# Attention in a two-layer backbone kernel: the weighted values of two query tiles in one fp32 product of 256 columns, turned probabilities in four places

## The reference

```
def block(qblk):
    s = jnp.einsum('bhgqd,bhkd->bhgqk', qblk, k_all).astype(jnp.float32) * scale
    pr = jax.nn.softmax(s, axis=-1).astype(v_all.dtype)
    return jnp.einsum('bhgqk,bhkd->bhgqd', pr, v_all)
...
y = jnp.concatenate([multiscale_pool(p[..., :D_POOL], pool_w, pool_scale), attn], axis=-1) @ w_out
```

## Time and profile before

| | us |
|---|---|
| time of three runs, median (lowest to highest) | 1564.88 (1564.79 to 1565.66) |
| time of the profiled execution | 1565.75 |
| its span (first to last instruction) | 1564.0 |
| PE busy in the span | 1544.2 |
| DVE busy | 1047.2 |
| ACT busy | 572.4 |
| attention stage, scores of tile 1 to the last weighted values | 1075.2 to 1155.5 |

### The profile page before, as it was taken

One profiled execution on the slowest core, in us unless ns is written; L12 is line 12 of the kernel. 1 busy time (PEld: TensorE's weight loads), 2 busy tenths in 40 slices (PEclk: granted clock), 3 DMA queues, 4 the chain that ended last, 5 costly groups with the idle time before them and its releaser, 6 DMA issues. The chain is left out here.

```text
span 1564.0 us, 21770 instructions
## 1 busy us (share of the span) xinstructions
PE 1544.2 (99%) x8590; PEld 1325.1 (85%) x8590; DVE 1047.2 (67%) x1567; ACT 572.4 (37%) x870; POOL 24.3 (2%) x66
## 2 busy tenths in 40 slices
PE   8999999999999999999999999998999999999998
PEld 5888888778898888888888888988988888888887
DVE  4999999888848784678626446877647543444346
ACT  5423224684722221122211225635646332322233
POOL 0000000220000000000000000000000000000000
PEclk9999999999999999999999999999999999999999
DMA  9632132125136453445333223340022323233232
GB/s 323 198 80 81 55 109 67 68 83 147 34 111 220 161 189 121 149 162 195 113 100 129 55 91 71 107 140 28 1 68 68 95 93 117 72 107 108 81 99 89
DMA packets 132746, 171.54 MB, mean 110 GB/s; under 512 B 16114, under 2 KB 88498, under 8 KB 132666
## 3 DMA queue, kind: packets, MB, share of 16 engines
q1 hardware_dynamic: 131770, 168.25, 33.7%
q0 software_dynamic: 640, 2.10, 0.3%
q10 hardware_dynamic: 256, 0.08, 0.0%
HBM read 166.17 MB, written 2.15 MB: 108 GB/s over the span
## 5 line engine op out<-in xcount | busy, mean ns | idle before, releaser
L741 PE MATMUL acc<-h_hi,w_hi 128*128 128x512 f32 (+1 forms) x1424 | 494.5, 351 | 0.0
L741 PE MATMUL acc<-h_lo,w_hi 128*128 128x512 f32 (+1 forms) x1424 | 492.4, 349 | 0.0
L741 PE MATMUL acc<-h_hi,w_lo 128*128 128x512 f32 (+1 forms) x1424 | 492.3, 349 | 0.0
L1757 DVE TENSOR_TENSOR w_lo<-raw,w_hi 128x1024 fp32r<-128x1024 f32 x183 | 218.1, 1219 | 131.9 <-ACT w_hi L1257 131.7
L741 PEld LDWEIGHTS acc<-h_hi,w_lo 128*128 128x128 f32 x1424 | 267.1, 189 | 35.0
L741 PEld LDWEIGHTS acc<-h_hi,w_hi 128*128 128x128 f32 x1424 | 267.3, 189 | 34.5
L741 PEld LDWEIGHTS acc<-h_lo,w_hi 128*128 128x128 f32 x1424 | 267.2, 189 | 33.8
L1257 ACT ACTIVATE w_hi<-raw 128x1024 fp32r<-128x1024 f32 x183 | 186.5, 1053 | 216.3 <-PE acc L790 150.7
L790 PE MATMUL acc<-w_hi,hid_hi 128*128 128x512 f32 x434 | 169.5, 391 | 0.0
L790 PE MATMUL acc<-w_hi,hid_lo 128*128 128x512 f32 x434 | 168.9, 389 | 0.0
L790 PE MATMUL acc<-w_lo,hid_hi 128*128 128x512 f32 x434 | 168.8, 389 | 0.0
(11 more groups left out here) (300 smaller groups left out, 2067.8 us busy)
## 6 DMA issues: line engine op xcount, KB each, us to landing
ada_w<-in_ada_w SPq DMA_DIRECT2D x96, 512.0 KB, 5.7
raw<-in_ffn_w_in SPq DMA_DIRECT2D x88, 512.0 KB, 3.6
raw<-in_ffn_w_out SPq DMA_DIRECT2D x44, 512.0 KB, 4.4
raw<-in_even_w_in SPq DMA_DIRECT2D x24, 512.0 KB, 4.5
ada<-in_ada_w SPq DMA_DIRECT2D x8, 1024.0 KB, 12.0
raw<-in_odd_w_in SPq DMA_DIRECT2D x12, 512.0 KB, 3.7
raw<-in_even_w_out SPq DMA_DIRECT2D x8, 512.0 KB, 5.9
raw<-in_odd_w_out SPq DMA_DIRECT2D x8, 512.0 KB, 4.0
```

The source lines that it names most:

```text
L741: last = nc.tensor.matmul(acc[:, s, m, t0:t1], w[:, slot, kk, c], x_[:, k, t0:t1], start=(k == 0 and q == 0), stop=(k == KD - 1 and q == 2))
L1757: return nc.vector.tensor_tensor(out_, in0, in1, op)
```

## The change

`weighted_values(n)` becomes `weighted_pair(p)`, which multiplies tiles 2p and 2p + 1 together: six fp32 products of 256 columns, whose streamed operand is two pieces of 128 columns from two neighbouring places of `pT`. It is issued only in even rounds from 2 on (pair n/2 - 1 behind the transposes of tile n), and once behind the loop. Odd rounds have none. `pT` gets four places, at another offset, and `turned_copy` and `head_high` wait by pairs. DVE's program, ACT's order and everything else are as they were.

```
-        pT = place("pT", [P, 2, T], offset=A0 + 74624)
+        pT = place("pT", [P, 4, T], offset=A0 + 52096)
...
-            def weighted_values(n):
-
-                hd, i = divmod(n, NL)
-                pe.wait_ge(sem("pT_ready"), n + 1)
+            def weighted_pair(p):
+
+                hd, i = divmod(2 * p, NL)
+                pe.wait_ge(sem("pT_ready"), 2 * p + 2)
                 if hd >= 2 and i == 0:
                     pe.wait_ge(h_ready, HEADS + hd - 1)
-                c = (hd % 2) * 512 + i * P
+                c, b = (hd % 2) * 512 + i * P, 2 * (p % 2)
+                dst = acc[:, 1, 1, c:c + 2 * P].rearrange("p (a t) -> p a t", t=P)
                 for j in range(NT):
-                    last = nc.tensor.matmul(acc[:, 1, 1, c:c + P], v1[:, j, (hd // 3) * HD:(hd // 3 + 1) * HD],
-                                            pT[:, n % 2, j * P:(j + 1) * P], start=(j == 0), stop=(j == NT - 1))
-                if n < N_Q * NL - 1:
+                    last = nc.tensor.matmul(dst, v1[:, j, (hd // 3) * HD:(hd // 3 + 1) * HD],
+                                            pT[:, b:b + 2, j * P:(j + 1) * P], start=(j == 0), stop=(j == NT - 1))
+                if p < N_Q * NL // 2 - 1:
                     last.then_inc(sem("pv_done"), 1)
                 return last
...
-                if n >= 1:
-                    weighted_values(n - 1)
-            last = weighted_values(N_Q * NL - 1)
+                if n >= 2 and n % 2 == 0:
+                    weighted_pair(n // 2 - 1)
+            last = weighted_pair(N_Q * NL // 2 - 1)
...
-                    act.wait_ge(sem("pv_done"), NL * (hd + 1))
+                    act.wait_ge(sem("pv_done"), NL // 2 * (hd + 1))
...
-                if n >= 2:
-                    act.wait_ge(sem("pv_done"), n - 1)
-                nc.scalar.activation(pT[:, n % 2, :], acc[:, 1, 0, 0:T], ACT.Copy).then_inc(sem("pT_ready"), 1)
+                if n >= 4:
+                    act.wait_ge(sem("pv_done"), n // 2 - 1)
+                nc.scalar.activation(pT[:, n % 4, :], acc[:, 1, 0, 0:T], ACT.Copy).then_inc(sem("pT_ready"), 1)
```

## The result

The changed kernel takes 1571.35 us (median of 6 runs, 1571.2 to 1571.81), the kernel before 1565.04 us beside it (1564.75 to 1565.66). The ratio is 1.004, with a 95% interval of 1.0029 to 1.005: slower by 6.3 us. The forecast was 1571.2 us.

The account below looks back on a forecast made before the run. PE was taken to bound the attention stage. Waits of 3.9 us in the middle, with the width's gain included, 1.25 at the start and 1.15 at the end summed to +6.3 us: 1571.2 us, range 1568.8 to 1573.5.

Parts of the forecast that it names:

- The rule of 2.18 us: Attention stage: the next transposes can start 2.18 us after the last ones started, through DVE, if scores stood directly ahead.
- The three terms: Attention stage: PE loses 3.9 us in the middle, 1.25 us at the start and 1.15 us at the end.
- the two chains: From one set of transposes to the next: 2.18 us through DVE's normalisation, 1.80 us through ACT's turned copy.
- the boldest single step: Stage start: tile 2's transposes wait for ACT's turned copy of tile 1, so start at 1084.24 in both kernels.
- The width: Weighted values: a pair in 256-column products takes 2.59 us instead of 2.68, 1.1 us gained over twelve pairs.
- The size of the waits in the profile: PE waits: nine of 0.4 to 0.5 us, about 1.5 us at tile 22, about 1.7 us at tile 2.
- Rival 1: Even transposes: DVE's chain fits, ACT's does not, leaving 0.09 us waits in the middle; 1567.3 us, chance 0.06.
- Rival 2: Whole stage: all waits are hidden and only the width counts; 1563.8 us, chance 0.04.
- Rival 3: Waits cost more: slow two-piece operand (up to +1.1 us) or a clock fall at the start (1575 us); chance 0.06.

Follow-up runs that it names:

- the exchange on DVE: Changed kernel with DVE normalising each even tile before taking the maximum of the next odd tile: 1567.15 us, ratio 1.0014.
- the one product put between: Changed kernel with one of a pair's six products moved between odd and even transposes, and head_high one round later: 1567.10 us, ratio 1.0014.
- the longer maximum: One more maximum on DVE per tile, over 384 of the scores: 1576.75 us in the changed kernel, 1567.03 us in the kernel before.
- the order alone: Changed kernel's order and four pT places, but weighted values again as products of 128 columns: 1572.39 us, ratio 1.0048.

## Why the prediction was right

**The rule of 2.18 us** was its centre, and the trace gives 2.19 (1107.71 to 1109.90). That DVE's order sets it is shown by the exchange on DVE, by the one product put between, and by the longer maximum, which costs nearly three times as much in one order as in the other.

**The three terms** can be read off the two chains. They are measured between ends of weighted values, in both traces, and the stage's beginning is taken out by counting from its first scores (1075.20 before, 1074.73 after).

| | predicted | before, us | after, us | difference |
|---|---|---|---|---|
| start of tile 2's transposes, from the first scores | same | 9.04 | 9.03 | 0.0 |
| from there to the end of the next weighted values | +1.25 | 2.19 | 3.44 | +1.25 |
| middle, to the end of the weighted values of tile 19 | +3.9 | 54.92 | 58.89 | +3.97 |
| end, to the last weighted values | +1.15 | 14.13 | 15.30 | +1.17 |
| sum | +6.3 | 80.28 | 86.66 | +6.4 |

The first scores came 0.47 us earlier in the trace of the changed kernel (1074.73), a difference from ahead of the stage, and behind the last weighted values both have the same rest (408.5 and 408.6 us). Hence the spans differ by 6.0 and not 6.4 us. That the forecast time missed the median by only 0.15 us is in part luck: the kernel before alone gave medians of 1564.88 to 1565.11 us, and its profiled execution 1565.75.

That the transposes of tile 2 start at the same point although 1.34 us of work has gone from in front of them was the boldest single step; the first row of the table and the version with single tiles at the start both bear it out. The chain of the changed kernel at its end, beside the earlier trace rows, has the 1.5 us in which PE waits; the transposes of tile 21 (1146.98 in the timeline) end at 1147.64:

```profile
1148.50 0.63 DVE ptile L2567
1149.13 0.04 issue
1149.17 0.88 PE acc L881 x6
1150.05 2.76 PE acc L790 x12
1152.80 2.59 PE acc L1217 x12
```

**The width** measured 2.59 us for a pair, as worked out from the contiguous records of another stage; the operand in two pieces costs nothing that can be seen. The 0.38 us that the prediction took for a record's own length is not in the rows it names; the trace of the kernel before has 0.378 us for records of 256 columns at line 997. Against the order alone the width gives 1.07 us in the traces. An estimate by the isolated gap in the Trainium skill's page "TensorE: Matmul & The Clock Gate", section "Back-to-back issue gap", would have been 0.03 x 12 = 0.4 us; the trace does not bear it out, and the row was the better guide for records of 128 columns.

**The size of the waits in the profile** was the step that I put wrongly. I said nine idle times of 0.4 to 0.5 us and one of 1.7 at tile 2; the profile prints 0.33 and 1.36. The stalls have the predicted length in PE's queue (0.48 us from 1.71 to 2.19), but the printed idle time begins only when the last matmul has left the pipeline. At tile 2 a wait of 0.27 us of the scores of tile 4 for the exponential, in the weight loads, is a further part. It changed nothing in the sum, which was made from distances between starts.

**The rivals.** Rival 1, ACT's chain in place of DVE's, was put at 1567.3 us; when DVE's order was changed so that it could come about, it gave 1567.15. That this is so close is chance in part: the rival left the end at +1.15 us, while in that run the transposes of tile 22 come 0.38 us sooner, and it had nothing for the 0.05 us by which a set that waited is longer. Rival 2 needed 0.47 us of PE work that the order didn't have; given 0.43 us, the nine stalls fell from 0.48 us to 0.05. Rival 3 did not come about: the granted clock stays 1.00 from 1080 to 1090 us, with 8.35 us of PE work in it. The longer wait at tile 2, 1.36 us, didn't bring the clock down. At another place it was nearer: with 0.47 us more of waiting at the first scores, which the change leaves alone, the clock did fall in the two runs with the longer DVE chain. Its price there was 0.1 to 0.4 us and not 4, since most of the slowed products lay beside DVE's chain.

## What to carry to other kernels

When work on the busiest engine is put together into larger pieces, ask what it stood between: here six small products helped to cover a chain through DVE that was 2.18 us long, and the 1.71 us of other work couldn't alone. For each pair of neighbouring instructions that the new order creates on the bound engine, add up the chain that links them through the other engines' queues, in those engines' own order, and compare it with the work left between them. And if a regrouping has a small gain of its own, give it back its cover by splitting the piece, not by undoing it.

## What the runs showed of the hardware

- PE's granted clock fell to its lower level for some 3.5 us behind a wait of 2.08 us (and 2.07 in the other run), with scores as the only work from there to the next wait; a wait of 1.61 us at the same place left it at the upper level in the kernel before and in the changed one. In both runs only the profiled execution shows it; where between these two waits it turns was not tried.
- A moving operand of two pieces of 128 fp32 columns, 3072 bytes apart in each partition, ran at the pace of a contiguous one of 256: 0.216 us a record (2.59 us for 12 in the changed kernel, for the other).
- Two maxima in a row on DVE cost less than their lengths: one of 384 columns takes 0.556 us by itself, but the next starts 0.47 us after it (1093.09 to 1093.56 in the kernel before with the longer chain). In the changed kernel with it PE's idle time grew by 0.46 us in two rounds (0.33 to 0.79).
